# A hybrid decoder trunk on one core: keys as second item, keys, stick-breaking rows and half of the norm turned through device memory

## The reference, cut to what matters

```python
h = rms_norm(x, attn_norm)
proj = h @ w_in                     # 1024 x 7428: pool, diff q k v, stick-breaking q k v, forgetting q k v, f, gates
y_n = branch_n(...) @ w_branch[rows of branch n]       # four causal mixers
x = x + (sum_n sigmoid(gate_n + b_gate_n) * y_n) @ w_out
h = rms_norm(x, ffn_norm)
x = x + (silu(h @ w_up[:, :2816]) * (h @ w_up[:, 2816:])) @ w_down
```

## Time and profile before

| what | value |
|---|---|
| median of 3 runs | 839.39 us (839.23 to 839.45) |
| the profiled execution's own time | 839.11 us |
| its span, first to last instruction | 837.3 us |
| granted TensorE clock over the span | 1.00 |
| busy: PE, DVE, ACT, POOL | 829.9, 632.5, 445.0, 119.6 us |
| DMA | 184.00 MB, mean 220 GB/s |

### The profile page before, as it was taken

How to read it: one execution, slowest core, us unless ns; L and a number is a source line. 1 busy time by engine, 2 the same in 40 slices (tenths; PEclk the granted TensorE clock), 3 DMA queues, 4 the chain that set the end, 5 groups by cost and what they waited for, 6 DMA issues and landing times.

```text
span 837.3 us, 11062 instructions
## 1 busy us (share of the span) xinstructions
PE 829.9 (99%) x4014; PEld 685.8 (82%) x4014; DVE 632.5 (76%) x932; ACT 445.0 (53%) x642; POOL 119.6 (14%) x89
## 2 busy tenths in 40 slices
PE   9999999999999999999999999999999999999998
PEld 7888778788888888888888887887888888888887
DVE  6898998799677676565479979978986776667543
ACT  7666746654554544444375666556643744444441
POOL 0751201008101000000005602010261000000000
PEclk9999999999999999999999999999999999999999
DMA  9867788686667777666566667887876587766651
GB/s 338 280 215 228 225 264 275 214 280 223 214 183 252 220 202 218 204 214 220 183 185 186 181 211 247 252 248 216 287 247 186 148 250 213 220 200 225 218 167 51
DMA packets 115334, 184.00 MB, mean 220 GB/s; under 512 B 18640, under 2 KB 39632, under 8 KB 115280
## 3 DMA queue, kind: packets, MB, share of 16 engines
q1 hardware_dynamic: 114848, 182.64, 69.9%
q10 hardware_dynamic: 432, 0.66, 0.3%
HBM read 167.52 MB, written 9.96 MB: 212 GB/s over the span
## 4 chain that ended last, share of the span: by engine, by line
PE 96%; DVE 1%; ACT 1%; issue 1%; DMA 1%; ACTq 0%; DVEq 0%
PE bulk L1835 30%; PE bulk L1839 30%; PE bulk L1836 30%; PE bankAB L1619 1%; DMA raw<-in_w_in_dram 1%; ACT wide L1043 0%; PE bulk L1882 0%; PE bulk L1863 0%; PE bankAB L1744 0%; PE bulk L1869 0%; PE bankO L1755 0%; PE bankAB L1628 0%; DVE keys_lo L1344 0%; DVE w_lo L1147 0%; PE bankO L1757 0%
## 5 line engine op out<-in xcount | busy, mean ns | idle before, releaser
L1147 DVE TENSOR_TENSOR w_lo<-raw,w_hi 128x1024 fp32r<-128x1024 f32 (+1 forms) x288 | 364.0, 1283 | 102.2 <-ACT w_hi L863 100.3
L863 ACT ACTIVATE w_hi<-raw 128x1024 fp32r<-128x1024 f32 (+1 forms) x286 | 296.3, 1047 | 229.6 <-PE bulk L1839 224.0
L1835 PE MATMUL bulk<-w_hi,hT_hi 128*128 128x512 f32 (+1 forms) x880 | 342.3, 389 | 0.7 <-DVE wide L1452 0.7
L1836 PE MATMUL bulk<-w_lo,hT_hi 128*128 128x512 f32 (+1 forms) x880 | 339.2, 385 | 0.0
L1839 PE MATMUL bulk<-w_hi,hT_lo 128*128 128x512 f32 (+1 forms) x880 | 336.2, 386 | 0.0
L1835 PEld LDWEIGHTS bulk<-w_hi,hT_hi 128*128 128x128 f32 x880 | 165.3, 188 | 34.5 <-DVE w_lo L1147 1.4
L1839 PEld LDWEIGHTS bulk<-w_hi,hT_lo 128*128 128x128 f32 x880 | 165.0, 188 | 33.2
L1836 PEld LDWEIGHTS bulk<-w_lo,hT_hi 128*128 128x128 f32 x880 | 165.3, 188 | 32.2
L1835 PE MATMUL bulk<-w_hi,aT_hi 128*128 128x512 f32 x174 | 67.8, 390 | 0.0
L1839 PE MATMUL bulk<-w_hi,aT_lo 128*128 128x512 f32 x174 | 67.7, 389 | 0.0
L1836 PE MATMUL bulk<-w_lo,aT_hi 128*128 128x512 f32 x174 | 67.7, 389 | 0.0
(11 more groups left out here) (233 smaller groups left out, 705.7 us busy)
## 6 DMA issues: line engine op xcount, KB each, us to landing
raw<-in_w_in_dram SPq DMA_DIRECT2D x110, 512.0 KB, 4.9
raw<-in_w_ffn_up_dram SPq DMA_DIRECT2D x80, 512.0 KB, 4.1
raw<-in_w_ffn_down_dram SPq DMA_DIRECT2D x44, 512.0 KB, 3.7
raw<-in_w_branch_dram SPq DMA_DIRECT2D x20, 512.0 KB, 6.2
raw<-in_w_out_dram SPq DMA_DIRECT2D x16, 512.0 KB, 3.5
wide<-wide SPq DMA_DIRECT2D x160, 32.0 KB, 2.7
bias<-in_b_gate_dram SPq DMA_DIRECT2D x16, 256.0 KB, 4.9
raw<-in_w_ffn_up_dram SPq DMA_DIRECT2D x16, 256.0 KB, 3.1
```

The lines of the kernel that those rows point to most:

```text
L863: act.activation(w_hi[:, g % RING, :, 0:width], raw[:, g % RAW, :, 0:width], ACT.Copy).then_inc(hi_ready, 1)
L1147: vec.tensor_tensor(w_lo[:, g % RING, :, 0:width], raw[:, g % RAW, :, 0:width], w_hi[:, g % RING, :, 0:width].bitcast(F32), ALU.subtract). ...
L1835: pe.matmul(dst, hi, whi, start=(k == ks[0]), stop=False)
L1836: pe.matmul(dst, hi, wlo, start=False, stop=False)
```

## The change

- `ITEMS`: `dk` moves ahead of `ss`, so `dk` has units 4 to 7 and `ss` 8 to 11.
- `tr_ss` and `tr_qk` are gone. `ss` and `dk` are turned by VectorE (slots 13 and 18) and go through device memory (slots 17, 18 and 22, 23 of SP), like `dq` (turn moved from 16 to 15, transfers from 20, 21 to 19, 20). ScalarE stages `ss` into `fox_gained`; the factor 1/8 moves from the queries into the sigmoids' scale.
- `sb_scores` 0 and 1 move from 14 and 20 to 21 and 23 on TensorE, the first differential scores from 25 to 26. Head norm of `dk`: ScalarE 14 to 9, VectorE 14 to 11.
- `down` runs interleaved for 8 tiles only, then item 0 to its end and item 1 to its end. So half 0 of x is finished 7 units before the layer's end (slot D0 = 137): residual, gain and the turn of half 0 of the next layer's norm run there, its rows go by device memory (slots 141, 142), and `tr_norm` remains for half 1 alone.

```diff
 ITEMS = [
     ("dq", "w_in", [(OFF["dq"], 512)], KD),
+    ("dk", "w_in", [(OFF["dk"], 512)], KD),
     ("ss", "w_in", [(OFF["sq"], 512)], KD),
-    ("dk", "w_in", [(OFF["dk"], 512)], KD),
...
-            for k in range(0, KF - 4, 2):
+            for k in range(0, DOWN_SPLIT, 2):
                 units += [(n, k), (n + 1, k)]
-            units += [(n, KF - 4), (n, KF - 2), (n + 1, KF - 4), (n + 1, KF - 2)]
+            for j in range(2):
+                units += [(n + j, k) for k in range(DOWN_SPLIT, KF, 2)]
...
-    (9, "tr_ss"), (14, "sb_scores", 0), (20, "sb_scores", 1), (24, "tr_qk", "dk"), (25, "scores", "diff", 0),
+    (21, "sb_scores", 0), (23, "sb_scores", 1), (26, "scores", "diff", 0), (30, "sb_out", 0), (30, "scores", "diff", 1),
...
-PE_MID = {0: [("tr_norm", "attn", 1, 0), ("tr_norm", "attn", 1, 1)],
+PE_MID = {0: [("tr_norm", "attn", 1, 1)],
...
-TURN_AT = {"dq": 16, "fox": 33, "diff": 48, "merged": 62}
+TURN_AT = {"ss": 13, "dq": 15, "dk": 18, "fox": 33, "diff": 48, "merged": 62}
-ROWS_AT = {"dq": (20, 21), "fox": (36, 37), "diff": (50, 51), "merged": (66, 68)}
+D0 = LAST[("down", 0)] + 1
+ROWS_AT = {"ss": (17, 18), "dq": (19, 20), "dk": (22, 23), "fox": (36, 37), "diff": (50, 51), "merged": (66, 68), "norm": (D0 + 4, D0 + 5)}
...
-    (4, "qk_norm", "dq"), (8, "ss"), (10, "ss_evac"), (11, "lambda_sums"), (14, "qk_norm", "dk"), (14, "sb_breaks", 0),
-    (19, "svfq"), (21, "fkfv"), (22, "sb_breaks", 1), (23, "qk_evac", "dq"), (24, "qk_evac", "dk"), (25, "dv"),
+    (4, "qk_norm", "dq"), (9, "qk_norm", "dk"), (11, "lambda_sums"), (12, "ss"), (18, "ss_evac"), (19, "svfq"),
+    (21, "sb_breaks", 0), (21, "fkfv"), (23, "qk_evac", "dq"), (24, "sb_breaks", 1), (24, "qk_evac", "dk"), (25, "dv"),
...
-    (3, "qk_sums", "dq"), (5, "row_mean"), (5, "qk_norm", "dq"), (7, "lambda_sums"), (7, "ss_evac"), (10, "lambdas"),
-    (14, "qk_norm", "dk"), (16, "turn", "dq"), (19, "sb_weights", 0), (19, "sb_turn", 0), (23, "qk_evac", "dq"),
+    (3, "qk_sums", "dq"), (5, "row_mean"), (5, "qk_norm", "dq"), (7, "lambda_sums"), (10, "lambdas"), (11, "qk_norm", "dk"),
+    (13, "turn", "ss"), (15, "turn", "dq"), (18, "turn", "dk"), (18, "ss_evac"), (22, "sb_weights", 0), (22, "sb_turn", 0),
...
             def norm_evac(layer, which, t, b):
+                if (which, b) == ("attn", 0):
+                    wait_spread(act, layer - 1, "norm")
+                    lhs_part(layer, ("norm", which, t, b), by_quads(hT[0], (0, 4), t), spread_columns("norm", t, (0, 4)))
+                    return
...
-                act.activation(stays[:, :, :], bankAB[:, :, 0:384], ACT.Sigmoid, scale=-1.0)
-                act.activation(breaks[:, :, :], bankAB[:, :, 0:384], ACT.Sigmoid).then_inc(sb_broken, 1)
+                act.activation(stays[:, :, :], bankAB[:, :, 0:384], ACT.Sigmoid, scale=-HD ** -0.5)
+                act.activation(breaks[:, :, :], bankAB[:, :, 0:384], ACT.Sigmoid, scale=HD ** -0.5).then_inc(sb_broken, 1)
...
-                        if u == U - 4 and layer + 1 < DEPTH:
-                            tr_norm(layer + 1, *PE_NEXT[1:])
```

More of the change, by code:

```diff
@@ L573, in build @@
         ff_ready = signal("ff_ready", [(p, t) for p in range(NPAIR + 1) for t in range(TT)])
-        turned_stages = list(TURN_AT) + [("act", p) for p in range(NPAIR + 1)]
+        turned_stages = list(TURN_AT) + [("act", p) for p in range(NPAIR + 1)] + ["norm"]
         spread_stages = [s for s in turned_stages if s not in BY_DRAM]
@@ L730, in _ @@
                             continue
+                        if stage == "norm" and layer + 1 == DEPTH:
+                            continue
                         turned, spread, blocks = turning(stage)
@@ L887, in head_squares @@
             def head_squares(layer, which):
+                if which == "dq" and layer:
+                    act.wait_ge(sumsq["attn"], nth(sumsq["attn"], layer, (1, 1)))
                 for t in range(TT):
@@ L905, in qk_norm @@
                 if which == "dk":
-                    act.wait_ge(stage_done, nth(stage_done, layer, ("tr_ss", 1)))
+                    act.wait_ge(normed, nth(normed, layer, ("dq", 1)))
                 head_squares(layer, which)
@@ L1214, in norm_evac @@
             def norm_evac(layer, which, t, b):
+                if (which, b) == ("attn", 0):
+                    lhs_rest(layer, ("norm", which, t, b), by_quads(hT[1], (0, 4), t), spread_columns("norm", t, (0, 4)),
+                             by_quads(hT[0], (0, 4), t))
+                    return
                 lhs_rest(layer, ("norm", which, t, b), hT[1][:, 4 * b:4 * b + 4, t * P:(t + 1) * P],
@@ L1490, in ff_up, with turn_blocks @@
                                              op1=ALU.mult).then_inc(ff_ready, 1)
-            def turn_blocks(layer, stage, ready, event, source):
-                vec.wait_ge(ready, nth(ready, layer, event))
+            def turn_blocks(layer, stage, ready, event, source, ahead=0):
+                vec.wait_ge(ready, nth(ready, layer + ahead, event))
                 turned, _, blocks = turning(stage)
@@ L1501, in turn @@
             def turn(layer, stage):
[L1503 to L1504 removed]
+                if stage == "norm":
+                    if layer + 1 < DEPTH:
+                        turn_blocks(layer, stage, hn_ready["attn"], (1, 0), lambda t: hn(t)[:, 0:NC], 1)
+                    return
+                if stage in ("dq", "dk"):
+                    turn_blocks(layer, stage, *(rotated, (stage, 1)), lambda t: xn(stage, t))
+                elif stage == "ss":
+                    turn_blocks(layer, stage, *(ss_staged, 1), lambda t: fox_gained[:, t, :])
                 elif stage == "fox":
@@ L1629, in tr_norm @@
                 ins.then_inc(stage_done, 1)
-            def tr_qk(layer, which):
-                for t in range(TT):
-                    pe.wait_ge(rotated, nth(rotated, layer, (which, t)))
-                    name = QK_BANKS[which][t]
-                    take(name, qkT_ready, layer, (which, t))
-                    for k in range(4):
-                        ins = pe.transpose(bank[name][:, k * P:(k + 1) * P], xn(which, t)[:, k * P:(k + 1) * P], identity)
-                    ins.then_inc(stage_done, 1)
             def tr_forget(layer):
@@ L1648, in tr_forget @@
                 ins.then_inc(stage_done, 1)
-            def tr_ss(layer):
-                for t in range(TT):
-                    pe.wait_ge(ss_staged, nth(ss_staged, layer, t))
-                    take("TO"[t], sT_ready, layer, t)
-                    for k in range(4):
-                        ins = pe.transpose(bank["TO"[t]][:, k * P:(k + 1) * P], scratch(t, SQ)[:, k * P:(k + 1) * P], identity)
-                    ins.then_inc(stage_done, 1)
             def cum(layer):
@@ L1899, in _ @@
                 while u < U:
-                    if layer == 0 and u == FIRST["dk"]:
+                    if layer == 0 and u == FIRST["ss"]:
                         pe.wait_ge(consts_loaded, 16)
```

104 lines of the change are left out of this document (43 added, 61 removed).

## The result

The changed kernel takes **854.0 us** (median, 853.26 to 854.61), the kernel before 839.36 beside it: ratio 1.0173, 95% interval 1.0159 to 1.0186. 853.5 was forecast. The profiled execution took 853.26 us, its span is 851.2.

A forecast was written before the change was run, and what follows sets the result against it. TensorE's instruction stream was taken as the bound. From 839.11 us, -4.4 (turns) + 7.5 + 6.2 (waits) + 4.2 (clock) + 0.6 (rest) = +14.1 gave 853.2, as a median 853.5 us; range 845.5 to 858.5.

The forecast's parts named there:

- The removed turns: 40 turn matmuls leave TensorE's path (stick-breaking rows, keys, norm at the layer border): -4.4 us.
- The wait for the product: At unit 12 TensorE waits for VectorE's head-norm product to free the keys' bank: +7.5 us layer 0, +6.2 layer 1.
- The clock: Behind each of the two new waits TensorE runs at half speed, half of 4.3 us lost twice: +4.2 us.
- The rest: Differential scores wait for device-memory rows and second stick breaks; VectorE queue fuller near slots 25 to 33: +0.6 us.
- The added trips: VectorE's block turns and device-memory writes and reads for rows, keys and norm are covered: nothing, uncovered a few us each.
- The faster one: Rival: head norm ready before unit 12 wants the bank (39.3 us, layer 0), only turns count: 835.0 us, chance 0.05.
- Almost in time: Rival: milder GpSimd interference, unit 12 waits of 1.7 and 2.8 us, clock stays: 840.1 us, no change, chance 0.09.
- The turns buy nothing: Rival: TensorE waits elsewhere as long as the removed turns took, forecast 4.4 higher: 857.9 us, chance 0.05.

The follow-up runs named there:

- the run with both edits: Changed kernel with the keys' head norm at VectorE slot 9 instead of 11 and GpSimd silent until its product is there: 844.46 us.

## Why the prediction was right

**The removed turns, -4.4.** Right: 0.90 and 0.93 us at unit 9, 0.91 at the border, 0.80 at unit 24 in each layer where the keys' turns went without the order of items, and the border alone moved the median by 1.0.

**The wait for the product, +7.5 and +6.2.** Right in place, releaser and size: 7.15 and 5.93 us by unit starts. The product started at 45.34 us, and I had it ready at 46.8; the first of the pair is written by about 46.0. The working was right too: the subtractions and lambda operations took 7.1 us where I had 8.1, the norm 5.5 to its first product where I had 5.0, and with GpSimd silent the unit started at 41.38, near the lower end of 40.95 that VectorE's work alone gave.

**The clock, +4.2.** Right in kind, a little high: 2.08 + 1.51 by unit starts, 3.3 when filled with products. Half of 4.3 us was right for layer 0, where the clock was low for 4.3 us after TensorE was back; in layer 1 it was 3 us. In both layers the clock fell during the wait, and that part costs nothing. One reading of the earlier trace rows was wrong: the counts of matmuls in the windows at the start include those that only overlap the window. By start times the warm-up matmuls come every 0.107 us up to 5.21 us and every 0.055 us from 5.30, so the 4.3 us stand; PEclk is 1.00 in these windows and doesn't show it.

**The rest, +0.6.** The weakest term. 14.6 us were measured between the medians; -4.5 + 13.1 + 3.6 leave +2.4. Between the two traces, 14.0 us apart, they leave +1.8: about 2.3 at units 33 and 52, both waits for VectorE, less the 0.6 us of waiting for the keys, which went. That the whole came within 0.5 us is partly luck: the two waits and the clock were 1.2 us too high together, this term 1.8 too low.

**The added trips, cost nothing.** Right for this kernel, and only for it. I named the cover as three units between ScalarE's slot 18 and the scores, and that was not it. The true cover was the wait at unit 12. Without that wait the rows cost 4.0 us at unit 20, which is neither their reader nor one that I had looked at: the price is paid through ScalarE's in-order queue by the bank of `svfq`. "A few us at most" was the right size. The price of the trip itself was too low: I took 3.4 us for a write, and in the changed kernel the rows' and the keys' take 5.0 and 6.6 (DMA issues: count, KB each, median us to landing):

```profile
rows_ss<-v_d SPq DMA_DIRECT2D x2, 512.0 KB, 5.0
rows_dk<-wide SPq DMA_DIRECT2D x2, 512.0 KB, 6.6
```

**The rivals.** The faster one had the right condition (the product before 39.3 us) and the wrong price: in the run with both edits the product was written by about 38.2 us and the time was 844.5, not 835.0. What was missing is that each wait hides the next. "Almost in time" took gaps of 1.7 and 2.8 us as short enough for the clock to stay; in these runs it fell after gaps of 2.69, 2.19 and 1.88 us. "The turns buy nothing" did not hold for the border, nor for the changed kernel as it is (854.0 where the order alone took 856.9), since the wait at unit 12 covered the trips. It held once that wait was gone: the keys' turns cost TensorE 0.8 us a layer, their trip 3.1 and 2.6 us of waiting. For the rows' turns by themselves it is open.

**Open.** Whether any table gets the whole 4.4 us. What remains in layer 0 is the chain of GpSimd's rotations and the keys' trip; moving the rotations to another engine wasn't tried. The rows' trip in the old order without the keys' wasn't run either.

## What to carry to other kernels

When items alternate between two banks, moving one forward moves the due time of whatever frees its bank by as much: here four units (10.9 us) against three slots on VectorE. Work moved off the busiest engine is free only while its latency has cover, and a wait elsewhere may be that cover; take the wait away before you call the trip free. In an in-order queue look at what stands behind a waiting entry, not only at its reader.

## What the runs showed of the hardware

A tiny VectorE operation beside GpSimd can wait as long as a whole GpSimd step: 0.17 us became 1.22 (L1167) and 1.13 (L1171), a 128x1 operation took 1.26. In the run with the head norm at slot 9 five of its thirteen small operations waited, one for each GpSimd step they met, and the norm took 7.8 us to its product where it took 3.9 with GpSimd silent. GpSimd's own steps kept their 0.7 and 1.3 us there, while beside a weight subtraction both sides suffer (2.27 instead of 1.23 us; a step 2.3 instead of 1.3). So the loss of a chain of small operations goes by the GpSimd steps it meets, not by the operations' size. The reductions (1.27 us a pair) and the block turns (1.29 a pair) kept their time beside GpSimd. The Trainium skill, SBUF — State Buffer, section "Who interferes with whom", calls the port pair that VectorE and GpSimd share an exclusive lock and excepts VectorE instructions with at most one SBUF input outside the 2-port modes; the rows agree.

The clock fell behind shorter gaps than I had rows for: after 2.69 us of idleness at unit 16 (1.64 us lost), after 2.19 us at unit 12 with GpSimd silent and after 1.88 us at unit 123 in the old order with the norm at slot 12, but not after 2.15 in the other layer of the run with GpSimd silent.
